# Last feed-forward: 9 of 22 gate-and-up jobs as seven block products, with weight block sums on GpSimd

## What is computed

```python
def conv_glu_ffn(h, w_up, conv_w, conv_b, w_down):     # h: 512 x 1024, w_up: 1024 x 5632, w_down: 2816 x 1024
    S = h.shape[1]
    a, b = jnp.split(h @ w_up, 2, axis=-1)
    a_pad = jnp.pad(a, ((0, 0), (CONV_WIDTH_2 - 1, 0), (0, 0)))
    a = sum(conv_w[j] * a_pad[:, j:j + S] for j in range(CONV_WIDTH_2)) + conv_b
    return (jax.nn.silu(a) * b) @ w_down
x = x + conv_glu_ffn(rmsnorm(x, g_ffn[i]), f_w_up[i], f_conv_w[i], f_conv_b[i], f_w_down[i])
```

## Time and profile before

| | us |
|---|---|
| median of 3 runs | 2093.96 (2092.58 to 2094.46) |
| the profiled execution, its own time | 2093.53 |
| its span | 2091.7 |
| PE busy | 2059.9 |
| DVE, ACT, POOL busy | 989.1, 885.9, 840.6 |
| ffn2_up0 | ends at 1859.44 |
| ffn2_up1 | ends at 2025.34 |

### The profile page before, as it was taken

The page is one execution under the profiler, slowest core; times in us unless marked ns, Lnnn a source line. Parts: engine busy times, 40 slices in busy tenths (PEclk is TensorE's granted clock), DMA queues, the critical chain, the costliest instruction groups (busy, mean ns, idle before and its releaser), DMA issues.

```text
span 2091.7 us, 28578 instructions
## 1 busy us (share of the span) xinstructions
PE 2059.9 (98%) x10618; PEld 1735.8 (83%) x10618; DVE 989.1 (47%) x1909; ACT 885.9 (42%) x1307; POOL 840.6 (40%) x273
## 2 busy tenths in 40 slices
PE   9999999999999999999999999999999999999998
PEld 6888977888888888876877888888887588888887
DVE  4889788574311111376985344034323934431432
ACT  3355545463443222534366453233423954432332
POOL 3443422444244444433713443444443044444443
PEclk9999999999999999999999999999999999999999
DMA  9654322325232432432202433333422034324322
GB/s 371 243 185 125 102 62 66 101 85 178 81 100 81 114 107 78 113 93 65 79 24 64 113 100 93 107 105 94 143 86 73 2 96 121 100 80 121 100 70 91
DMA packets 304008, 220.17 MB, mean 105 GB/s; under 512 B 13520, under 2 KB 288080, under 8 KB 301616
## 3 DMA queue, kind: packets, MB, share of 16 engines
q1 hardware_dynamic: 293216, 195.67, 31.1%
q10 hardware_dynamic: 10704, 23.33, 3.7%
HBM read 213.48 MB, written 2.10 MB: 103 GB/s over the span
## 4 chain that ended last, share of the span: by engine, by line
PE 85%; DVE 7%; issue 3%; ACT 2%; POOL 2%; DMA 0%; ACTq 0%; DVEq 0%; SPq 0%; POOLq 0%
PE bank L912 72%; PE bank L1159 2%; PE bank L1375 2%; PE bank L1353 2%; DVE arena L2811 1%; PE bank L1307 1%; DVE small L2809 1%; PE bank L1362 1%; PE bank L1458 1%; PE bank L1207 1%; POOL w_split_out L2851 1%; DVE bank L2277 1%; POOL w_split L2851 1%; PE bank L1218 1%; PE bank L1540 1%
## 5 line engine op out<-in xcount | busy, mean ns | idle before, releaser
L912 PE MATMUL bank<-h_hi,w_split 128*128 128x512 f32 x3696 | 1119.4, 382 | 1.8 <-DVE arena L2679 1.1
L2851 POOL TENSOR_TENSOR w_split<-wslots,w_split 128x2048 fp32r<-128x2048 f32 (+3 forms) x174 | 712.7, 4097 | 987.9 <-ACT w_split L1613 549.5
L912 PEld LDWEIGHTS bank<-h_hi,w_split 128*128 128x128 f32 x3696 | 698.7, 189 | 116.8 <-issue 15.7
L912 PE MATMUL bank<-h_lo,w_split 128*128 128x512 f32 x1848 | 701.8, 380 | 0.0
L912 PEld LDWEIGHTS bank<-h_lo,w_split 128*128 128x128 f32 x1848 | 349.7, 189 | 51.2 <-issue 3.4
L912 PE MATMUL bank<-hid_hi,w_split 128*128 128x512 f32 x1056 | 316.2, 380 | 2.2 <-DVEq L2562 2.2
L1634 ACT ACTIVATE w_split<-wslots 128x2048 fp32r<-128x2048 f32 (+2 forms) x80 | 141.4, 1767 | 368.0 <-PE bank L912 368.0
L1613 ACT ACTIVATE w_split<-wslots 128x2048 fp32r<-128x2048 f32 (+3 forms) x91 | 158.8, 1745 | 300.8 <-PE bank L912 278.9
L912 PEld LDWEIGHTS bank<-hid_hi,w_split 128*128 128x128 f32 x1056 | 199.6, 189 | 32.3 <-issue 3.6
L912 PE MATMUL bank<-hid_lo,w_split 128*128 128x512 f32 x528 | 200.1, 379 | 0.0
L2277 DVE SCALAR_TENSOR_TENSOR bank<-arena,cols,bank 128x512 f32<-128x512 f32 x240 | 161.3, 750 | 5.4 <-ACT bank L1727 4.9
(11 more groups left out here) (341 smaller groups left out, 2352.4 us busy)
## 6 DMA issues: line engine op xcount, KB each, us to landing
wslots<-in_f_w_up SPq DMA_DIRECT2D x88, 512.0 KB, 4.7
wslots<-in_w_in SPq DMA_DIRECT2D x24, 1024.0 KB, 5.3
wslots<-in_w_ffn_up SPq DMA_DIRECT2D x44, 512.0 KB, 4.5
arena<-in_w_ada ACTq DMA_DIRECT2D x8, 2048.0 KB, 9.1
wslots<-in_f_w_down SPq DMA_DIRECT2D x16, 768.0 KB, 4.8
wslots<-in_a_w_in SPq DMA_DIRECT2D x10, 1024.0 KB, 5.2
wslots<-in_f_w_down SPq DMA_DIRECT2D x16, 640.0 KB, 4.4
arena<-in_w_ada_first SPq DMA_DIRECT2D x8, 1024.0 KB, 19.3
```

Of the source, the lines that this page charges most:

```text
L912: return nc.tensor.matmul(bank[:], w, woven(x), start=start, stop=stop)
L2851: last = nc.gpsimd.tensor_tensor(part[:, 1, cols_of], slot(p, 1, size)[:, 0, cols_of], part[:, 0, cols_of].bitcast(F32), ALU.subtract)
```

## The change

In ffn2_up0 and ffn2_up1, the jobs on buffer set Q (the first of each pair), except for the first pair of either half, are computed as seven block products. That is 5 + 4 = 9 of the 22 jobs. The product of a job is taken as a 2x2 block matrix (gate and up tile by two halves of the features) times another (two halves of the features by two halves of the tokens). Seven products of half-sized blocks, each of 4 x 3 matmuls of 128x256, replace the eight that a plain product has. The operands are sums of blocks, and so are the results:

- **Token operands**, once per feed-forward: ACT copies 16 blocks of 128x256 from xT with the norm's gain, DVE makes four sums of 128x1024 (token_sums_made), ACT rounds each (128x1024) and POOL makes each lower part (128x1024).
- **Weight operands**, for each of the 9 jobs: POOL makes four block sums of 128x512 (weight_sums). ACT rounds seven entries of 128x512, four sums and three plain blocks (entry_uppers), and POOL makes seven lower parts (entry_lowers). The 128x2048 split of that job goes. The other job of the pair keeps its own.
- **Result sums**, for each: ACT copies 128x256 out of bank 6 (first_product), DVE does 128x256 and 128x512 (early_sums), then 128x512 and twice 128x256 (late_sums) ahead of the seven steps.
- **Order.** On ACT, entry_uppers for the next seven-product job stands ahead of the convolution of the present job on set Q. In the other job of the pair the convolution now stands ahead of the weight split. On POOL, each turn is entry_lowers of this pair, lower_weights of this pair's other job, then weight_sums for the next pair. In the first pair of ffn2_up0 the four token lower parts stand between the plain lower parts and the first weight_sums. PE starts a seven-product job on bank_free[Q].
- A tiny silu at the head of ACT's loop, up_acc placed over up_gate, some semaphores shared under new names, and another operand for the idle matmuls at the end.

```diff
         up_gate = region(2, T)
-        up_acc = region(2, T)
+        up_acc = up_gate
...
+        HALF = T // 2
+        BLOCK = DT * P
+        entry_at = [unused.pop(), square_at, -(-(cons_at + 4 * EARLY_CONSTS) // 32) * 32] + [arena_at + 4 * (w_split_at + BLOCK * (4 * Q + k)) for k in range(4)]
+        entries = [split_at(f"entry{e}", [P, 2, DT // 2, P], at) for e, at in enumerate(entry_at)]
...
+            def seven_products(name, half, i, use):
+                unit = unit_of(half, i)
+                pe.wait_ge(bank_free[Q], use + 1)
+                for e, (bank, at, tokens) in enumerate(((7, 0, 3), (7, 1, 1), (6, 1, 2), (2 * Q, 1, "h22"), (6, 0, "h11"), (2 * Q, 0, "h21"), (2 * Q + 1, 0, 4))):
+                    if e < 6:
+                        pe.wait_ge(S["sums_lower"], unit * 6 + (TOKEN_SUMS + e + 1))
+                    else:
+                        pe.wait_ge(lo_ready[Q], SPLITS_BEFORE[FIRST[name]] + i + 1)
+                    for c in range(DT // 2):
+                        for wp, hp in ((0, 0), (0, 1), (1, 0)):
...
+                            last = nc.tensor.matmul(banks[bank][:, at * HALF:(at + 1) * HALF], entries[e][:, wp, c, :], x,
+                                                    start=c == 0 and wp + hp == 0, stop=c == DT // 2 - 1 and wp == 1)
+                    if e == 4:
+                        last.then_inc(S["g_turned_then_products"], 1)
+                last.then_inc(product_done[Q], 1)
...
+            def entry_uppers(name, half, i):
+                unit = unit_of(half, i)
+                for e, made in enumerate((1, 3, 4, 4)):
+                    act.wait_ge(S["angle_then_sum_ready"], unit * 4 + (SUMS_FIRST + TOKEN_SUMS + made))
+                    nc.scalar.activation(entries[e][:, 0, :, :], entry_sum(e), ACT.Copy).then_inc(S["softplus_then_sums_upper"], 1)
+                act.wait_ge(weights_in[Q], weights_of(name, 0, i))
+                act.wait_ge(product_done[Q], i + FIRST[name] // 2)
+                for e, (m, k) in ((4, (0, 0)), (5, (0, 1)), (6, (1, 1))):
+                    nc.scalar.activation(entries[e][:, 0, :, :], block_of(m, k), ACT.Copy).then_inc(S["softplus_then_sums_upper"] if e < 6 else hi_ready[Q], 1)
...
+            def mixed_ahead(name, half, take, conv):
...
+                def turn(i, u, p, use):
+                    if u == 0:
+                        entry_uppers(name, half, i + 1)
+                        conv(i, u, p, use)
+                    else:
+                        conv(i, u, p, use)
+                        act.wait_ge(weights_in[p], weights_of(name, u, i + 1))
+                        nc.scalar.activation(w_split[p][:, 0, 0:size], slot(p, 1, size)[:, 0, :], ACT.Copy).then_inc(hi_ready[p], 1)
+                    take(i, u, p, use)
...
                 for i, u, p, use in pairs(act, name, 1, turns - 1):
+                    if u == 0:
+                        nc.scalar.activation(small[:, 121:122], con("eps", 1), ACT.Silu)
+                        first_product(half, i)
+                    turn(i, u, p, use)
...
             late_root_act(act, "ffn2")
+            for c in range(DT):
+                for n in range(2):
...
+                    last = nc.scalar.activation(block[:, c0:c0 + 2, :], halves(xT[:, c, :])[:, :, n * P:(n + 1) * P], ACT.Copy, scale=late_gain("ffn2", c))
+                if c % (DT // 2) == DT // 2 - 1:
+                    last.then_inc(S["softplus_then_sums_upper"], 1)
+            for j, made in ((2, 2), (0, 3), (1, 4), (3, 4)):
+                act.wait_ge(S["angle_then_sum_ready"], SUMS_FIRST + made)
+                nc.scalar.activation(token_sums[j][0][:], token_sum(j), ACT.Copy).then_inc(S["softplus_then_sums_upper"], 1)
             ffn(2)
...
+            def early_sums(half, i):
...
+                steps.did(nc.vector.tensor_tensor(second_sum, banks[6][:, right], first_and_fourth[:, left], ALU.add))
...
+                steps.did(nc.vector.tensor_tensor(third_and_fourth, both, banks[7][:].rearrange("p (a b) -> p a b", a=2), ALU.add))
+            def late_sums(use):
+                dve.wait_ge(product_done[Q], use + 1)
...
+                steps.did(nc.vector.tensor_tensor(banks[2 * Q][:], banks[2 * Q][:], first_and_fourth, ALU.add))
+                up = banks[2 * Q + 1]
+                steps.did(nc.vector.tensor_tensor(up[:, 0:HALF], up[:, 0:HALF], third_sum, ALU.add))
+                steps.did(nc.vector.tensor_tensor(up[:, HALF:], banks[7][:, HALF:], third_sum, ALU.add))
...
+            def token_sums_made():
...
+                def sum_of(j, a, b):
+                    nc.vector.tensor_tensor(token_sum(j), token_sum(a), token_sum(b), ALU.subtract).then_inc(S["angle_then_sum_ready"], 1)
...
+            def entry_lowers(name, half, i):
...
+            def weight_sums(half, i, first=False):
...
+                if not first:
+                    pool.wait_ge(S["g_turned_then_products"], unit + 1)
+                pool.wait_ge(weights_in[Q], weights_of(name, 0, i))
...
+                sum_of(0, block_of(0, 0), block_of(1, 0), ALU.subtract)
+                sum_of(1, block_of(1, 0), block_of(1, 1), ALU.add)
+                made(2)
+                sum_of(2, entry_sum(1), block_of(0, 0), ALU.subtract)
+                if first:
+                    pool.wait_ge(product_done[Q], one(name, 0)[1] + 1)
+                made(3)
+                sum_of(3, block_of(0, 1), entry_sum(2), ALU.subtract)
+            def mixed_weights(half):
+                name = f"ffn2_up{half}"
+                split_weights(name, first="turn")
+                if half == 0:
+                    for n, j in enumerate((2, 0, 1, 3)):
+                        pool.wait_ge(S["softplus_then_sums_upper"], 1 + 2 + n + 1)
+                        nc.gpsimd.tensor_tensor(token_sums[j][1][:], token_sum(j), token_sums[j][0][:].bitcast(F32), ALU.subtract).then_inc(S["sums_lower"], 1)
+                turns = JOBS[name] // 2
+                weight_sums(half, 1, True)
+                for i, u, p, use in pairs(pool, name, 1, turns - 1):
+                    if u == 0:
+                        entry_lowers(name, half, i)
+                    else:
+                        lower_weights(name, p, SPLITS_BEFORE[FIRST[name] + u] + i)
+                        weight_sums(half, i + 1)
```

More of the change, by code:

```diff
@@ L1171, in _ @@
                                                    con("ident", HEADS, HEADS))
-                    last.then_inc(S["g_turned"], 1)
+                    last.then_inc(S["g_turned_then_products"], 1)
             def tile_product(k, between=None):
@@ L1567, in idle_products @@
                 for _ in range(n):
-                    nc.tensor.matmul(banks[7][:], con("one"), trig[:, 0, :], start=True, stop=True)
+                    nc.tensor.matmul(banks[7][:], con("one"), wslots[:, 0:T], start=True, stop=True)
             before = TILES_BEFORE["last"]
@@ new lines, in mixed_turns @@
+            def mixed_turns(half, tiles, turn):
+                name, turns = f"ffn2_up{half}", tiles // 2
+                for i, u, p, use in turn_of(name, 0):
+                    turn(i, u, p, use)
+                for i, u, p, use in pairs(dve, name, 1, turns - 1):
+                    if u == 0:
+                        steps.loop(i + (-1), 7)
+                        early_sums(half, i)
+                        late_sums(use)
+                    turn(i, u, p, use)
+                steps.end_loop(turns - 2)
+                for i, u, p, use in turn_of(name, turns - 1):
+                    if u == 0:
+                        early_sums(half, i)
+                        late_sums(use)
+                    turn(i, u, p, use)
@@ L2755, in ffn, with turn @@
                     w3, _ = conv3_of(k, t0, tiles)
-                    for i, u, p, use in pairs(dve, f"ffn{k}_up{half}"):
-                        if u == 0:
-                            steps.loop(i, 2)
+                    def turn(i, u, p, use):
                         t = 2 * i + u
@@ L2773, in ffn @@
                         hidden(n, t, tiles, p, use)
-                    steps.end_loop(tiles // 2)
+                    if k == 2:
+                        mixed_turns(half, tiles, turn)
+                    else:
+                        for i, u, p, use in pairs(dve, f"ffn{k}_up{half}"):
+                            if u == 0:
+                                steps.loop(i, 2)
+                            turn(i, u, p, use)
+                        steps.end_loop(tiles // 2)
                     if half == 0:
@@ L2869, in ffn @@
+            def ffn(k):
+                if k == 2:
+                    for half in range(2):
+                        mixed_weights(half)
+                        split_weights(f"ffn2_down{half}")
+                    return
                 split_weights(*(name for name, _ in ffn_stages(k)))
```

145 lines of the change are left out of this document (125 added, 20 removed).

## The result

The changed kernel takes **2123.99 us** (median of 4 runs, 2121.63 to 2124.83) against 2094.21 for the kernel before in the same set of runs: a ratio of 1.0137, 95% interval 1.0120 to 1.0155. On 2094.21 us that ratio is +28.7, its interval +25.1 to +32.5 (the two medians differ by 29.8). It is slower, near the predicted 2122. The profiled execution took 2123.3 us, its span is 2121.5 us, 29.8 longer than before.

The account below looks back on a forecast made before the run. PE, busy 98%, bounds the kernel before; after, a 22.0 us cycle without PE. ffn2_up0 +24.9, ffn2_up1 +2.8 and clock +0.5 make +28.2 on 2093.53: 2121.7, median 0.4 above, so 2122; range 2115 to 2133.

Parts of the forecast that it names:

- The pair's cycle: Loop through DVE, ACT and POOL in each pair: 22.0 us without PE, against PE's 19.73, so PE waits 2.3.
- Step by step, in my order: DVE to convolution 0.95, to split 0.68, to POOL 1.99, lower part 4.56, sums 5.42, roundings 2.75, convolution to DVE's end 5.56, turn 0.1.
- The start of ffn2_up0: Token operands precede the first convolution: PE idles 20.8 us, and with the later cycles this half loses 24.9 us.
- the clock: Half-clock spells after PE's stalls, mainly the first: 0.5 us in all, bounds 0 to 3.
- The start of ffn2_up1: No stall at the second half's start; with its cycles of 22.0 us this half loses 2.8 us.
- The collision: At ffn2_up0's start, a DVE token sum and POOL's token parts hold each other up: 1.2 us, bounds 0 to 2.6.
- The sum: Whole kernel: 24.9 + 2.8 + 0.5 = +28.2 us on 2093.53, 2121.7; median forecast 2122.
- A sign that failed: In the changed profile, PE's matmul busy time was to fall by 8 to 9 us while the span grows.
- That PE stays the bound: Rival: PE still sets the ffn2 up halves, 9 jobs save 8.9 us, time 2085; 5%.
- Only the start stalls: Rival: ffn2_up0's start stalls but the pair's cycle fits under PE, needing 2.3 us less: +11.9, 2106; 8%.
- The late weights: Rival: slot Q's weight transfers queue, 3.2 us more in each of 7 cycles, 2145; 7% including a low-clock variant.
- a clock that stays down through whole pairs: Added to late weights in the ffn2 up pairs: 36 us more, 2158; 7% for both together.

Follow-up runs that it names:

- the repeat: The changed kernel, unaltered, run and profiled a second time: 2123.57 us (one run).
- the second experiment: On top of the version with ACT's convolution first, the first job's silu and rounding also go ahead of the first entries in either half: 2110.32 us, 1.0071.
- the version with 7 units: Convolution first, token operands made piecewise in plain pairs, seven-product jobs from pair 3 of ffn2_up0, 7 instead of the change's 9: 2092.76 us, 0.9989 times before.

## Why the prediction held

**The pair's cycle**, predicted 22.0, measured 21.75. Step by step, in my order: 0.95, 0.67, 1.99, 4.50, 5.24, 2.66, 5.52 and 0.22 against 0.95, 0.68, 1.99, 4.56, 5.42, 2.75, 5.56 and 0.1. Of the 0.18 on the sums' side 0.14 is POOL's waits for its own results: the gaps between its sums are 0.08 and 0.08, not 0.15 each. That this chain, and not PE, sets the pair is shown from three sides: half of PE's work in a unit taken away leaves the 21.7 us, 1.28 us more on POOL lengthens it, and the convolution moved ahead of the roundings shortens it to PE's 19.7. PE's waits for bank_free, predicted as 2.3 us in each pair, are 1.6 on average; the cycle is 2.0 over PE's 19.73, and the waits view counts less, since a matmul row ends later than the next could begin (0.38 us long at a distance of 0.22).

**The start of ffn2_up0**, predicted a stall of 20.8 us, measured 20.0. ACT's sixteen copies took 6.42 us (predicted 6.1), the four lower parts with the collision 10.27 (10.6), the sums and roundings from 1766.08 to 1774.00 7.9 (8.2), and the last steps 5.25 (5.56). In half 0 as a whole, the last job's end moves from 1859.44 to 1887.43. Less the 3.48 us that the root is late, that is **+24.5** against +24.9. In it the first cycle is 22.9 us, 1.2 above the others, because PE ran at half clock: POOL waited 1.30 us for its fifth product, and with half the matmuls the cycle was 21.6. I had put 0.5 on the clock in a term of its own, so with it my sum for this half was 25.4, 0.9 too much.

**The start of ffn2_up1**: no stall, as predicted. Its first scaling to its last takes 95.5 us against 93.2: **+2.2** against +2.8, the four cycles being 21.6, 21.7, 21.7 and 20.0.

**The collision**, predicted 1.2 us. With the two apart, POOL gained 1.04. It was as forecast one DVE sum standing for POOL (3.34 us instead of 1.23) and one part of POOL standing for that sum (3.35 instead of 2.34). The Trainium skill, "SBUF — State Buffer", "Who interferes with whom", says that a DVE instruction with two SBUF inputs contends with a GpSimd instruction that reads SBUF, and that the port pair they share is an exclusive lock; the rows with and without overlap agree (5.86 against 3.74 us on DVE).

**The sum.** 24.5 + 2.2 = 26.7 us belong to ffn2, against my 28.2. The profiled spans differ by 29.8, the ratio gives 28.7. The profiled execution has 3.5 us ahead of the root, in code that the change leaves as it was. The term was not in my sum, and it made my total look closer than its parts are; that much is luck. Two half-clock spells of 3.4 us, at half speed about 1.7 us each, are as large. The repeat shows one of them absent; there the root is 2.4 us late and ffn2 loses 28.1 us. So ffn2's loss itself moves by 1.4 us between two executions, and both are within the interval of the ratio (25.1 to 32.5).

**A sign that failed.** I wrote that PE's matmul busy time would fall by 8 to 9 us. It fell by 1.7 us over the span and by 4.7 us in the up halves. The saving is there all the same: with the convolution first a pair takes 19.74 us, 0.98 less than 20.72. But busy time counts the half clock (1779.25 to 1783.7 is 4.4 us, of which 2.2 are loss), the two spells, and the long ends of the rows ahead of each wait.

**The rivals.** That PE stays the bound (2085) was wrong for this order. With the convolution first it is right for the cycle, but its time was never reached, since the start still stalls. "Only the start stalls" (2106) describes that version, 2106.46. Its condition, 2.3 us less in each cycle, did not need faster sums, only another place for the convolution. The late weights (2145) cost the change nothing, but cost the second experiment its gain. The 36 us for a clock that stays down through whole pairs have no working in the prediction; outside the start, the longest spell seen in ffn2 in the two profiles of the change is under 4 us.

## What to carry to other kernels

- When work of another engine is put ahead of a step that frees a buffer, add up the loop from that step back to itself, through every in-order queue. If the sum is over the bound engine's own time, each turn pays the difference, however idle the engines look. POOL's 44% is a mean over the whole span; in a pair it is busy for 18.5 of 22 us.
- One-time operands are best made in the gaps of turns that run anyway. Here the operands made in one piece came with a stall of 20 us (19 with the convolution first), and spread out they came with none, which was worth giving up 3 of the 9 cheaper jobs.

## What the hardware showed beyond that

The clock did not come back with the work. In the changed kernel it fell at about 1763.2, 4.0 us after PE had stopped (1759.2), and rose at about 1783.7, 4.4 us after PE had started again (1779.25). The windows:

```profile
1762.00:1764.00 2.00, 0.00 (x0) 0.00 (x0) 0.00 (x0) 0.00 (x0) 2.00 (x2) 0.80 0.00 0
1764.00:1779.00 15.00, 0.00 (x0) 0.00 (x0) 2.84 (x4) 7.14 (x11) 14.78 (x12) 0.50 0.00 0
1779.00:1782.00 3.00, 2.75 (x13) 2.76 (x14) 2.52 (x5) 2.02 (x2) 0.82 (x1) 0.50 0.19 50
1782.00:1784.00 2.00, 2.00 (x12) 2.00 (x12) 1.02 (x2) 1.17 (x3) 1.36 (x1) 0.58 1.13 328
1784.00:1786.00 2.00, 2.00 (x20) 2.00 (x19) 0.69 (x1) 0.60 (x2) 2.00 (x1) 1.00 0.50 121
```

Short waits went either way. In the first profile of the change four later waits of 6.0 us in all in ffn2_up0, and three in ffn2_up1 with a longest of 1.9, left the clock at 1.00; in the repeat the same wait of 1.9 us was followed by 0.57 from 1992 to 1996. In the kernel with one more sum the four later waits of ffn2_up0 (7.9 us in all) each came with a spell (0.93 over each pair). A stall thus can cost more than its length: 3.0 us of waiting in the version with 7 units came with a clock of 0.50 behind it, 1.7 us more.
